# First block's front: four projection units on the input before its norm, the inverse root multiplied in at the gated join

## The reference, cut to what matters

```python
h = rmsnorm(x, norm_mix[i])                 # x * rsqrt(mean(x*x) + eps) * gain
z = h @ w_in[i]
u, qf, kvf, ng, mg = jnp.split(z, splits, axis=-1)
a = u[..., :D_CONV] * jax.nn.sigmoid(u[..., D_CONV:])
a = causal_dwconv(a, conv_dw_w[i], conv_dw_b[i])
a = jax.nn.silu(layernorm(a, conv_ln_g[i], conv_ln_b[i]))
y_conv = a @ w_conv_out[i]
```

## Time and profile before

| | |
|---|---|
| median of three runs | 4018.65 us |
| profiled execution: its span, first to last instruction | 4012.6 us |
| TensorE busy | 3861.1 us (96%) |
| VectorE busy | 2292.9 us (57%) |
| ScalarE busy | 1328.5 us (33%) |
| GpSimd busy | 1346.3 us (34%) |
| DMA: share of the 16 engines by the loads of queue 1 | 24.5% |

### The profile page before, as it was taken

One profiled execution on the slowest core, in us unless ns is written; L12 is line 12 of the kernel. 1 busy time (PEld: TensorE's weight loads), 2 busy tenths in 40 slices (PEclk: granted clock), 3 DMA queues, 4 the chain that ended last, 5 costly groups with the idle time before them and its releaser, 6 DMA issues. The chain is left out here.

```text
span 4012.6 us, 63599 instructions
## 1 busy us (share of the span) xinstructions
PE 3861.1 (96%) x26755; PEld 3054.9 (76%) x26755; DVE 2292.9 (57%) x3310; ACT 1328.5 (33%) x2136; POOL 1346.3 (34%) x554
## 2 busy tenths in 40 slices
PE   8999999999999999988889999999999999999998
PEld 6866788867678887577776788778777787877886
DVE  5756567487667755578874776555550626252034
ACT  3356333243223333444443433322232111103222
POOL 1011444443234441000001544445554343654442
PEclk9999999999999999999999999999999999999999
DMA  5311222323122222531102222212212112222221
GB/s 178 129 61 40 87 105 84 110 108 109 60 84 87 101 105 106 187 117 51 59 28 87 84 105 95 96 68 84 84 63 78 62 66 86 94 105 84 87 102 63
DMA packets 43519, 359.87 MB, mean 90 GB/s; under 512 B 4323, under 2 KB 4707, under 8 KB 23948
## 3 DMA queue, kind: packets, MB, share of 16 engines
q1 hardware_dynamic: 43276, 356.35, 24.5%
HBM read 333.79 MB, written 22.28 MB: 89 GB/s over the span
## 5 line engine op out<-in xcount | busy, mean ns | idle before, releaser
L364 POOL TENSOR_TENSOR ffn_weights_low<-weight_ring,ffn_weights_high 128x2048 fp32r<-128x2048 f32 x128 | 591.4, 4621 | 785.3 <-ACT ffn_weights_high L469 784.6
L211 PE MATMUL banks<-ffn_in_high,ffn_weights_low 128*128 128x512 f32 x2048 | 801.3, 391 | 10.9 <-POOL ffn_weights_low L364 8.9
L213 PE MATMUL banks<-ffn_in_high,ffn_weights_high 128*128 128x512 f32 x2048 | 798.8, 390 | 0.0
L212 PE MATMUL banks<-ffn_in_low,ffn_weights_high 128*128 128x512 f32 x2048 | 798.8, 390 | 0.0
L211 PEld LDWEIGHTS banks<-ffn_in_high,ffn_weights_low 128*128 128x128 f32 x2048 | 385.2, 188 | 97.3 <-POOL ffn_weights_low L364 11.4
L212 PEld LDWEIGHTS banks<-ffn_in_low,ffn_weights_high 128*128 128x128 f32 x2048 | 385.2, 188 | 79.8 <-issue 0.7
L213 PEld LDWEIGHTS banks<-ffn_in_high,ffn_weights_high 128*128 128x128 f32 x2048 | 385.2, 188 | 79.6
L469 ACT ACTIVATE ffn_weights_high<-weight_ring 128x2048 fp32r<-128x2048 f32 x128 | 245.2, 1915 | 558.4 <-PE banks L213 558.4
L623 DVE SCALAR_TENSOR_TENSOR ffn_gate<-ffn_up,columns_sb,ffn_gate 128x511 f32<-128x511 f32 (+1 forms) x132 | 273.0, 2068 | 160.7 <-ACT ffn_value L513 160.7
L4015 POOL TENSOR_TENSOR third_weights_low<-weight_ring,third_weights_high 128x1024 fp32r<-128x1024 f32 x144 | 359.6, 2497 | 11.5
L4013 POOL CAST third_weights_high<-weight_ring 128x1024 fp32r<-128x1024 f32 x144 | 158.8, 1103 | 513.5 <-PE banks L213 485.5
(11 more groups left out here) (673 smaller groups left out, 7544.7 us busy)
## 6 DMA issues: line engine op xcount, KB each, us to landing
weight_ring<-weights SPq DMA_DIRECT2D x143, 2048.0 KB, 7.7
scan_in<-rwkv_operands SPq DMA_DIRECT2D x7, 1280.0 KB, 6.0
rwkv_operands<-rwin_staged SPq DMA_DIRECT2D x23, 256.0 KB, 3.3
scan_in<-rwkv_operands SPq DMA_DIRECT2D x8, 512.0 KB, 3.9
bias_tiles<-bias_rows SPq DMA_DIRECT2D x8, 448.0 KB, 8.6
residual<-x SPq DMA_DIRECT2D x4, 512.0 KB, 7.2
hyena_u_x_T<-decay SPq DMA_DIRECT2D x2, 1024.0 KB, 7.9
rwkv_residual<-residual SPq DMA_DIRECT2D x1, 2048.0 KB, 7.1
```

What stands on the lines that cost most here:

```text
L211: pe.matmul(out, w[1], x[0], start=start, stop=False, skip_group_check=True)
L212: pe.matmul(out, w[0], x[1], start=False, stop=False, skip_group_check=True)
L213: return pe.matmul(out, w[0], x[0], start=False, stop=stop, skip_group_check=True)
L364: pool.tensor_tensor(parts[1], landed, parts[0].bitcast(F32), ALU.subtract).then_inc(S["split"], 1)
```

## The change

The loads come in another order: eight columns of gains first (`first_gains`, 32 bytes per partition), then the first pair of `x` tiles, the weights of unit 0, the other `x` tiles, the weights of unit 1, those of units 2 and 3, and the other columns. Units 0 to 3 multiply `x` times gain without the root (`raw_parts`, split by ScalarE and VectorE). These parts lie in the memory of the bias tiles, so the loads of these wait until four units are done (`tile_done` at `RAW`). The squares lie in the memory of the normed tiles. The sum of squares stands behind unit 0 on TensorE, two spreads of the root (banks 7 and 6) behind unit 1, and the lookup behind unit 2. ScalarE keeps a copy of the root (`root_kept`). VectorE multiplies it onto the gate's operand before the sigmoid, and the one in bank 7 onto the gate after it; then the join is as before. Normed tiles are used from unit 4 on. The weight splits of units 0 and 1 are both on VectorE now.

```diff
+    RAW = 4
...
-        x_squared = T.W[:, :, :].rearrange("p h n -> p (h n)")[:, 0:KT * SEQ].rearrange("p (k n) -> p k n", k=KT)
+        x_squared = G.hT
...
             x = G.aps["x"].rearrange("(k p) n -> p k n", p=P)
             sp.dma_start(G.const[:, :], G.aps["constants"]).then_inc(S["constants"], 16)
+            gains = G.layout["columns"]["norm_mix"][0]
+            assert gains == 0
+            sp.dma_start(G.cols[:, 0:KT], G.aps["columns"][:, 0:KT]).then_inc(S["first_gains"], 16)
             sp.dma_start(G.x[:, 0:2, :], x[:, 0:2, :]).then_inc(S["x_0"], 16)
+            sp.dma_start(G.ring[:, 0, 0:UNIT], G.weights[0][:, 0:UNIT]).then_inc(S["first_unit"], 16)
             sp.dma_start(G.x[:, 2:4, :], x[:, 2:4, :]).then_inc(S["x_1"], 16)
             sp.dma_start(G.x[:, 4:6, :], x[:, 4:6, :]).then_inc(S["x_2"], 16)
             sp.dma_start(G.x[:, 6:8, :], x[:, 6:8, :]).then_inc(S["x_3"], 16)
-            sp.dma_start(G.ring[:, 0, 0:UNIT], G.weights[0][:, 0:UNIT]).then_inc(S["first_unit"], 16)
-            sp.dma_start(G.cols[:, :], G.aps["columns"]).then_inc(S["columns"], 16)
-            sp.dma_start(G.ring[:, 0, UNIT:CHUNK], G.weights[0][:, UNIT:CHUNK]).then_inc(G.landed[0], 16)
+            sp.dma_start(G.ring[:, 0, UNIT:2 * UNIT], G.weights[0][:, UNIT:2 * UNIT]).then_inc(S["second_unit"], 16)
+            sp.dma_start(G.ring[:, 0, 2 * UNIT:CHUNK], G.weights[0][:, 2 * UNIT:CHUNK]).then_inc(G.landed[0], 16)
+            sp.dma_start(G.cols[:, KT:], G.aps["columns"][:, KT:]).then_inc(S["columns"], 16)
             sp.dma_start(onehot, G.aps["buckets"]).then_inc(S["onehot"], 16)
             sp.dma_start(G.ring[:, 1, :], G.weights[1]).then_inc(G.landed[1], 16)
             sp.wait_ge(S["rows_done"], 2)
             for c in range(COPIES):
                 sp.dma_start(rows_dram.ap()[:, c, :], rows).then_inc(S["stored"], 16)
             sp.wait_ge(S["stored"], 16 * COPIES)
-            sp.wait_ge(S["summed"], 1)
+            sp.wait_ge(S["tile_done"], RAW)
...
             first = G.first
-            sp.wait_ge(S["split_second"], 1)
-            G.feed(sp, 1, S["split_by_pool"], base=2)
+            sp.wait_ge(S["split_raw"], 2)
+            G.feed(sp, 1, S["split_by_pool"], base=1)
...
-            for n in (0, *range(2, BY_POOL), OUT, OUT + OUT_UNITS):
+            for n in (*range(2, BY_POOL), OUT, OUT + OUT_UNITS):
...
-            for k in range(2, KT - 1):
-                pe.wait_ge(S["squared"], k + 1)
-                keep_running(pe, G, 6, 1)
-            pe.wait_ge(S["square_added"], KT - 1)
-            for j in range(JT):
-                mm = pe.matmul(G.banks[:, 5, j:j + 1], rstd[:, j * P:(j + 1) * P], G.con("ones")[:, 0:1], start=True, stop=True)
-            mm.then_inc(S["summed"], 1)
-            pe.wait_ge(S["rstd_done"], 1)
-            root_spread(pe, G, 7, S["spread"])
+            keep_running(pe, G, 6, 4)
 
             def split(n):
-                if n == 1:
-                    pe.wait_ge(S["split_second"], 1)
+                if n < 2:
+                    pe.wait_ge(S["split_raw"], n + 1)
                 elif n < BY_POOL:
-                    pe.wait_ge(S["split_by_pool"], max(n, 1))
+                    pe.wait_ge(S["split_by_pool"], n - 1)
                 else:
                     pe.wait_ge(S["split_by_dve"], n + 1 - BY_POOL)
 
             def unit(n, bank, ready=None):
                 split(n)
                 w = parts(n)
+                rows_of = T.raw_parts if n < RAW else T.h_parts
...
-                    mm = exact_product(pe, G.banks[:, bank, :], [x[:, k, :] for x in w], [x[:, k, :] for x in T.h_parts],
+                    mm = exact_product(pe, G.banks[:, bank, :], [x[:, k, :] for x in w], [x[:, k, :] for x in rows_of],
...
+                    pe.wait_ge(S["gate_scaled"], 2)
...
-                unit(n, n % 8, S["h_split"] if n == 0 else None).then_inc(S["tile_done"], 1)
+                unit(n, n % 8, {0: S["raw_split"], RAW: S["h_split"]}.get(n)).then_inc(S["tile_done"], 1)
                 if n == 0:
+                    pe.wait_ge(S["square_added"], KT - 1)
+                    for j in range(JT):
+                        mm = pe.matmul(G.banks[:, 5, j:j + 1], rstd[:, j * P:(j + 1) * P], G.con("ones")[:, 0:1], start=True, stop=True)
+                    mm.then_inc(S["summed"], 1)
+                if n == 1:
+                    pe.wait_ge(S["rstd_done"], 1)
+                    root_spread(pe, G, 7, S["spread"])
+                    root_spread(pe, G, 6, S["second_spread"])
+                if n == 2:
+                    pe.wait_ge(S["root_kept"], 1)
                     pe.wait_ge(S["columns"], 16)
                     pe.wait_ge(S["onehot"], 16)
...
-            for k in range(KT):
+            def raw(k):
                 if k % 2 == 0:
                     act.wait_ge(S[f"x_{k // 2}"], 16)
+                act.activation(T.raw_parts[0][:, k, :], G.x[:, k, :], ACT.Copy, scale=G.col("norm_mix", k)).then_inc(S["raw_high"], 1)
+
+            def square(k):
                 act.activation(x_squared[:, k, :], G.x[:, k, :], ACT.Square).then_inc(S["squared"], 1)
 
             def high(n):
-                if n == 0:
-                    act.wait_ge(S["first_unit"], 16)
+                if n < 2:
+                    act.wait_ge(S["second_unit" if n else "first_unit"], 16)
                 elif n == OUT:
                     arrived(act, CONV_OUT)
                 elif n == OUT + OUT_UNITS:
                     arrived(act, MG_2)
-                elif n < OUT and (n == 1 or n % 4 == 0):
+                elif n < OUT and (n == 2 or n % 4 == 0):
                     arrived(act, chunk_of(n))
                 top, rest, whole = halves(n)
                 act.activation(top, whole, ACT.Copy).then_inc(S["rounded"], 1)
 
-            act.wait_ge(S["mean_done"], 1)
-            act.activation(G.roots[:, :], G.roots[:, :], ACT.Sqrt).then_inc(S["root_done"], 1)
+            act.wait_ge(S["first_gains"], 16)
+            raw(0)
+            raw(1)
             high(0)
-            for k in range(KT):
-                act.wait_ge(S["h_ready"], k + 1)
-                act.activation(T.h_parts[0][:, k, :], G.hT[:, k, :], ACT.Copy).then_inc(S["h_high"], 1)
-                if k == 5:
+            raw(2)
+            raw(3)
+            square(0)
+            raw(4)
+            raw(5)
+            square(1)
+            raw(6)
+            raw(7)
+            for k in range(2, KT):
+                square(k)
+                if k == 3:
                     high(1)
+
+            def gate(t):
+                if t >= 2:
+                    act.wait_ge(S["glu_done"], t - 1)
+                    act.activation(sg[:, t % 2, :], G.banks[:, 2 * t + 1, :], ACT.Sigmoid).then_inc(S["gate_done"], 1)
+                else:
+                    act.wait_ge(S["gate_rooted"], t + 1)
+                    act.activation(sg[:, t, :], sg[:, t, :], ACT.Sigmoid).then_inc(S["gate_done"], 1)
+
             for n in range(18):
                 act.wait_ge(S["tile_done"], n + 1)
-                high(n + 2)
+                if n != 2:
+                    high(n + 2)
                 if n == 0:
+                    act.wait_ge(S["mean_done"], 1)
+                    act.activation(G.roots[:, :], G.roots[:, :], ACT.Sqrt).then_inc(S["root_done"], 1)
+                if n == 1:
+                    act.wait_ge(S["second_spread"], 1)
+                    act.activation(rstd[:, :], G.banks[:, 6, :], ACT.Copy).then_inc(S["root_kept"], 1)
+                    for k in range(KT):
+                        act.wait_ge(S["h_ready"], k + 1)
+                        act.activation(T.h_parts[0][:, k, :], G.hT[:, k, :], ACT.Copy).then_inc(S["h_high"], 1)
+                        if k == 3:
+                            act.wait_ge(S["tile_done"], 3)
+                            high(4)
+                if n == 2:
                     for c in range(2):
                         act.wait_ge(S["looked_up"], c + 1)
                         act.activation(rows[:, c * 512:(c + 1) * 512], G.banks[0:HEADS, 5 + c, :], ACT.Copy, scale=-1.0)\
                            .then_inc(S["rows_done"], 1)
-                if n < 8 and n % 2:
-                    if n >= 4:
-                        act.wait_ge(S["glu_done"], n // 2 - 1)
-                    act.activation(sg[:, n // 2 % 2, :], G.banks[:, n, :], ACT.Sigmoid).then_inc(S["gate_done"], 1)
+                if n in (3, 4, 5, 7):
+                    gate((3, 4, 5, 7).index(n))
...
+            def raw_low(k):
+                dve.wait_ge(S["raw_high"], k + 1)
+                dve.scalar_tensor_tensor(out=T.raw_parts[1][:, k, :], in0=G.x[:, k, :], scalar=G.col("norm_mix", k),
+                                         in1=T.raw_parts[0][:, k, :].bitcast(F32), op0=ALU.mult, op1=ALU.subtract).then_inc(S["raw_split"], 1)
+
+            def weights_low(n):
+                dve.wait_ge(S["rounded"], n + 1)
+                top, rest, whole = halves(n)
```

(29 more changed lines are left out.)

## The result

The changed kernel is slower: 4036.51 us median of five runs (4035.43 to 4046.17) against 4017.04 of the kernel before in the same set. The ratio is 1.0047, with an interval of 1.0035 to 1.0059, so +18.9 us (14 to 24). The forecast was +12.7, a time of 4031.4 and a range up to 4034.5: right in sign and in place, too small in size. The profiled execution spans 4034.8, 22.2 more than the one before.

A forecast was written before the change was run, and what follows sets the result against it. TensorE's unbroken stream bounds the kernel, unit 8 waiting for chunk 2 behind the table's stores: +11.2 at unit 8 plus +1.5 slow clock is +12.7 on 4018.65, so 4031.4 us, range 4024 to 4034.5.

The forecast's parts named there:

- The date of the table: End of the table's two copies (`rows_done`), which lets the stores start: 44.0 in place of 32.28, +11.7 us.
- the slow stretch behind the pause: TensorE at unit 8: the 14.3 us pause brings 3.1 us at half speed, +1.5 us.
- What decides: SyncE's list started by `rows_done`: stores, bias loads, then chunk 2, which holds unit 8; unit 8 starts +11.2 us.
- The bias tiles' wait for four units: SyncE, before the bias loads: over at 45.1 and costs nothing, as the stores last to 55.5.
- TensorE's own clock, 3.1 ahead at unit 7's end: TensorE's stream before unit 8: unit 7 ends at 66.9 instead of 70.00, 3.1 us ahead.
- Date of the sum and unit 1: Front: additions end at 22.5, TensorE pauses 3.5 us, 1.3 added for half speed, unit 1 from 23.6 to 30.4.
- The tiles, 11.5 from first normed tile to last high part: Eight normed tiles before the table: from 31.5 to the last high part at 43.0, formerly 10.1 us.
- Chunk 2 at its old distance from the stores: SyncE and DMA: chunk 2 issued at 60.8 and landed at 78.9, 11.7 us after its old 67.16.
- The slack of 0.5: Before unit 8 in the old kernel: chunk 2 came 0.5 us before it would have stalled TensorE.
- The sum: Total of the forecast terms for the whole kernel: +11.2 at unit 8 and +1.5 at half speed, +12.7 us.
- Rival 3: TensorE's stream holds a second hole behind the pause, or its clock falls twice: +15, 4034 to 4037; 7%.
- The ends that I gave to the clock and to VectorE's pace: Uncertainties: clock at unit 1 -1.4 to +0.2, at unit 8 -1.5; input split +0.3 at most; tile-chain waiting 0 to 2.
- the low ends: All uncertain terms of the forecast taken at their lowest together: total loss +8 us, against +14 at the high ends.

The follow-up runs named there:

- chunk_first: Changed kernel with weight chunk 2 issued ahead of the bias table's stores and bias tile loads on SyncE; ratio to the kernel before 1.0001 (0.9992 to 1.0010).
- before_lookup_late: Kernel before with the bias table lookup behind unit 2 instead of unit 0, nothing else changed; ratio to the kernel before 1.0032 (1.0019 to 1.0045).
- lookup_early: Changed kernel with the lookup in TensorE's pause behind unit 0, ahead of the sum; ratio to the kernel before 1.0023 (1.0014 to 1.0032).
- before_chunk_first: Kernel before with weight chunk 2 issued ahead of the table's stores on SyncE; ratio to the kernel before 0.9998 (0.9988 to 1.0007).
- two_units_first: Changed kernel with chunk 2 ahead of the stores, unit 1 and the lookup before the sum, spreads after unit 2; ratio to the kernel before 0.9987 (0.9978 to 0.9996).
- pool_eighth: Changed kernel with GpSimd's subtractions for units 2 to 5 cut to the first of eight pieces; one run, 4038.71 us.
- warm_pause: Changed kernel with nine more fp32 warming matmuls while TensorE waits for the sum behind unit 0; ratio to the kernel before 1.0031 (1.0019 to 1.0043).

## Why the prediction was right or wrong, by its own steps

The forecast's mechanism and sign held; what failed were sizes. The date of the table was put at +11.7 and came at +15.6, as unit 1 at half speed and VectorE's tile chain beside GpSimd were taken too short, and the slow stretch behind the pause was put at +1.5 and cost +2.6. Point by point:

- **What decides** was right: `rows_done`, then stores, bias tiles, chunk 2, unit 8. chunk_first takes the loss away, before_lookup_late makes it anew. The bias tiles' wait for four units was right at nothing, and lookup_early shows what it costs once the other is gone.
- **TensorE's own clock, 3.1 ahead at unit 7's end**: measured 0.5 (ScalarE sees it at 69.55 in chunk_first, against 70.00; against before_chunk_first, where it sees it at 67.69, the changed front is 1.9 behind). The start of unit 0 was right (10.84 against 11.1), and so was that TensorE would pause for the sum. What was too small stands in the next point.
- **Date of the sum and unit 1.** Forecast: additions done 22.5, unit 1 from 23.6 to 30.4. Measured: 23.4, 25.17 to 32.83, and the first normed tile at 33.92 instead of 31.5: 2.4 late. The unit 0 that ran at full clock ended at 16.6, not 19, so the pause was 6.8 us and not 3.5; the slow stretch behind it took 6.2 us, in which the sum's matmuls cost 1.87 instead of 0.95 and unit 1 2.2 more than its 5.45. I had added 1.3 for all of it. The additions lost 1.9 to GpSimd; ScalarE's list, done at 18.35 instead of 19.5, made this good in part.
- **The tiles, 11.5 from first normed tile to last high part**: measured 13.0 (33.92 to 46.95). The step counted what ScalarE waits for and not GpSimd's subtraction of unit 4, which the change puts beside VectorE's low parts: +1.8 in one instruction. The kernel before had shown the size of a short meeting, at the first low part: GpSimd worked from 17.58 to 19.93, and the part took 0.95 where the others took 0.68.

```profile
17.58 2.35 POOL L919 TENSOR_TENSOR first_weights_low<-weight_ring,first_weights_high 128x1024 fp32r<-128x1024 f32 x1 [17.13 <-ACT first_weights_high L1090]
19.53 0.95 DVE L1206 TENSOR_TENSOR first_in_low<-normed,first_in_high 128x512 fp32r<-128x512 f32 x1
```

The longer tile chain (+1.5) and the point before it (+2.4) are the 3.9 by which +11.7 became +15.6.

- **Chunk 2 at its old distance from the stores**: 35.4 against 34.9, right within 0.6.
- **The slow stretch behind the pause, +1.5**: unit 8 ran from 85.82 to 94.05, 8.2 in place of 5.45, +2.6 when the 0.2 by which ScalarE sees an end late is left out. I took the 3.1 us of the earlier trace rows for the length of such a stretch; here it was 5.3.
- **The slack of 0.5** was read from ScalarE's start at 70.00; TensorE began unit 8 at 69.81, 0.33 after VectorE's half was done. With the chunk 16.2 later it began 16.0 later, so 0.2 of slack was used up.
- **The sum** of the terms as measured: stores +15.6, distance to the chunk +0.6, less 0.2 of slack, so that unit 8 starts 16.0 late (85.82 against 69.81), and +2.6: 18.6, as the trace has it, where the runs have 18.9. Rival 3's time, 4034 to 4037, holds the result, and the clock did fall twice, though at unit 1 and at unit 8, where my own sum had it too; a second hole behind unit 8 isn't there: from unit 8 on nothing more was lost. The ends that I gave to the clock and to VectorE's pace were each drawn from rows in which no pause was longer than 2.6 us and GpSimd met VectorE only for a moment; that made the range too narrow. Two slips of the working changed little: two spreads from 30.4 end at 32.7, not 32.5 (measured, they took 1.95 together), and the low ends add up to +6.9, not +8.

## What to carry to other kernels

Before moving a small step later, follow what is queued behind its semaphore on the engine that issues the loads, up to the first transfer that the busy engine needs, and read that transfer's slack (0.2 to 0.3 us here). A start that comes 10 us earlier is worth nothing while the list of loads behind it keeps its order: here it cost 19 us, and one load moved ahead gave all of it back. When work is put between two engines anew, look at what the third does at that time: VectorE operations stood still behind GpSimd four times in 32 us.

## What the runs showed of the hardware

- After a pause of 6.8 us TensorE worked at granted 0.50 for 6.2 us, after one of 16.3 for 5.3, after one of 2.6 for 3.1, and in two_units_first after one of 1.8 for some 3.4 (46.0 to 49.5). Before unit 0, pauses of 2.1 us (pool_eighth, two_units_first) were followed by a slow stretch of some 3.4 us each, and ones of 2.9 and 3.2 (warm_pause, lookup_early) by none. The price of a pause isn't read from one such stretch. Where the pause was filled (warm_pause) the clock stayed at 1.00.
- VectorE's subtraction, addition and plain copy of SBUF operands are held until about the end of the GpSimd subtraction that they meet: 0.69 us of work became 2.46. Normed tiles, which read PSUM, kept 0.70 each beside one (33.92 to 35.3 with GpSimd at work from 34.16).
- The first loads of the same instructions landed up to 2.3 us apart: unit 0 began at 20.63 in the kernel before and at 18.31 in before_chunk_first, and everything up to unit 8 moved with it.
- The same instructions from unit 8's end to the last took 3932 to 3947 us in nine profiled executions; single spans of this program can't tell less than that apart.
